# Coefficient transposes between the halves of the first MLP's first product, and two PSUM banks for the first product alone

## The reference

```python
def sq_relu_mlp(h, w1, w2):
    return jnp.square(jax.nn.relu(h @ w1)) @ w2

def second_block(x, ...):
    for layer in range(DEPTH):
        h = rms_norm_2(x, mix_norm_g[layer])
        ...
        x = x + sq_relu_mlp(rms_norm_2(x, ffn_norm_g[layer]), w_ff1[layer], w_ff2[layer])
```

## Time and profile before

| | us |
|---|---|
| median of 3 runs | 957.22 |
| lowest and highest run | 956.55, 960.41 |
| the profiled execution | 959.83 |
| its span, from first to last instruction | 958.0 |
| PE busy | 891.9 |
| DVE busy | 597.5 |
| ACT busy | 440.9 |
| POOL busy | 128.4 |

### The profile page before, as it was taken

How to read it: one execution, slowest core, us unless ns; L and a number is a source line. 1 busy time by engine, 2 the same in 40 slices (tenths; PEclk the granted TensorE clock), 3 DMA queues, 4 the chain that set the end, 5 groups by cost and what they waited for, 6 DMA issues and landing times.

```text
span 958.0 us, 12089 instructions
## 1 busy us (share of the span) xinstructions
PE 891.9 (93%) x5003; PEld 738.2 (77%) x5003; DVE 597.5 (62%) x704; ACT 440.9 (46%) x581; POOL 128.4 (13%) x73
## 2 busy tenths in 40 slices
PE   3999999898999999989999999998689989999997
PEld 2888778787887887787777888886677878888886
DVE  3595384675243765867697787886584565555453
ACT  5444375557853655343634444343126364444441
POOL 1000000211000011105054544441000000000000
PEclk9999999999999999579999999998779999999999
DMA  9625365363023642404545655554966555555521
GB/s 348 211 100 209 112 250 176 123 229 132 1 65 115 244 143 88 176 1 157 173 154 198 207 184 192 177 198 121 182 216 214 180 176 176 176 177 186 196 99 44
DMA packets 66784, 155.87 MB, mean 163 GB/s; under 512 B 2937, under 2 KB 6618, under 8 KB 66474
## 3 DMA queue, kind: packets, MB, share of 16 engines
q1 hardware_dynamic: 63424, 145.37, 45.0%
q0 software_dynamic: 2224, 7.67, 2.3%
q10 hardware_dynamic: 1082, 2.07, 1.0%
HBM read 146.70 MB, written 7.34 MB: 161 GB/s over the span
## 4 chain that ended last, share of the span: by engine, by line
PE 80%; DVE 10%; ACT 3%; issue 3%; DMA 2%; POOL 1%; ACTq 0%; DVEq 0%; POOLq 0%
PE bank L617 23%; PE bank L619 22%; PE bank L618 22%; PE bank L610 2%; PE bank L714 1%; DMA vrows<-in_vecs 1%; PE bank L872 1%; POOL rsh L1948 1%; DVE wlo L1385 1%; DVE wlo L1380 1%; DMA work<-x 1%; PE bank L755 1%; PE bank L687 1%; DVE aux L1558 1%; PE bank L976 1%
## 5 line engine op out<-in xcount | busy, mean ns | idle before, releaser
L1385 DVE TENSOR_TENSOR wlo<-ring,whi 128x2048 fp32r<-128x2048 f32 (+1 forms) x106 | 252.5, 2388 | 161.9 <-ACT whi L1062 161.8
L1062 ACT ACTIVATE whi<-ring 128x2048 fp32r<-128x2048 f32 (+1 forms) x106 | 202.3, 1910 | 234.9 <-PE bank L619 210.4
L617 PE MATMUL bank<-whi,hT_hi 128*128 128x512 f32 (+1 forms) x736 | 290.0, 394 | 5.8 <-DVE hT_lo L1368 4.1
L619 PE MATMUL bank<-whi,hT_lo 128*128 128x512 f32 (+1 forms) x736 | 287.7, 391 | 0.0
L618 PE MATMUL bank<-wlo,hT_hi 128*128 128x512 f32 (+1 forms) x736 | 287.5, 391 | 0.0
L617 PEld LDWEIGHTS bank<-whi,hT_hi 128*128 128x128 f32 x736 | 139.3, 189 | 35.2 <-DVE wlo L1385 2.8
L619 PEld LDWEIGHTS bank<-whi,hT_lo 128*128 128x128 f32 x736 | 139.2, 189 | 28.6
L618 PEld LDWEIGHTS bank<-wlo,hT_hi 128*128 128x128 f32 x736 | 139.3, 189 | 27.8
L617 PE MATMUL bank<-whi,hidT_hi 128*128 128x512 f32 x256 | 101.5, 396 | 1.1 <-DVE hidT_lo L1855 1.1
L619 PE MATMUL bank<-whi,hidT_lo 128*128 128x512 f32 x256 | 100.2, 392 | 0.0
L618 PE MATMUL bank<-wlo,hidT_hi 128*128 128x512 f32 x256 | 100.2, 391 | 0.0
(11 more groups left out here) (266 smaller groups left out, 998.6 us busy)
## 6 DMA issues: line engine op xcount, KB each, us to landing
ring<-in_w_ff SPq DMA_DIRECT2D x64, 1024.0 KB, 5.3
ring<-in_a_w_in SPq DMA_DIRECT2D x8, 1024.0 KB, 8.3
ring<-in_ple_gate_w SPq DMA_DIRECT2D x8, 1024.0 KB, 5.1
ring<-in_w_kv SPq DMA_DIRECT2D x8, 1024.0 KB, 6.4
ring<-in_b_w_in SPq DMA_DIRECT2D x8, 1024.0 KB, 5.1
ring<-in_w_in SPq DMA_DIRECT2D x6, 1024.0 KB, 5.6
ring<-in_w_glu SPq DMA_DIRECT2D x6, 1024.0 KB, 5.1
ring<-in_a_w_out SPq DMA_DIRECT2D x4, 1024.0 KB, 5.3
```

The costliest lines, as they stand in the source:

```text
L617: pe.matmul(bank_cols, high[:, at[0], at[1]], w_high, start=first, stop=False)
L619: return pe.matmul(bank_cols, low[:, at[0], at[1]], w_high, start=False, stop=last)
L1062: act.activation(whi[at], raw_rows(g), ACT.Copy).then_inc(high_made, 1)
L1385: dve.tensor_tensor(wlo[at], raw_rows(g), whi[at], ALU.subtract).then_inc(low_made, 1)
```

## The change

In the plan, the transposes of the hidden rows always go to banks 4 and 5, in both layers, and f1 to banks 6 and 7. In layer 0, wT goes to banks 4 and 5 as well (6 and 7 in turn 8), ahead of f1 in the count, and the taps to 4 and 5. PE runs the eight wT transposes between the two halves of f1, by the argument `between`, and the taps behind f1 as before. ACT copies wT out ahead of the two ReLUs, no longer behind the cast for f1's second half. DVE, POOL and SP keep their order.

```diff
--- before.py
+++ after.py
@@ -237,14 +237,16 @@
     for i in range(FB + 1):
         if i:
             for k in range(2):
-                u.add(("fT", layer, i - 1, k), "av")
+                u.add(("fT", layer, i - 1, k), "av", bank=4 + k)
+        if layer == 0 and i:
+            for k in range(2):
+                u.add(("wT", i - 1, k), "a", bank=(4 if i < FB else 6) + k)
         if i < FB:
-            gemm(u, ("f1", layer, i), 1, "v")
+            for t in range(NT):
+                u.add((("f1", layer, i), 0, t), "v", bank=6 + t)
         if layer == 0 and i:
-            u.add(("wT", i - 1, 0), "a")
-            u.add(("wT", i - 1, 1), "a")
-            u.add(("taps", i - 1, 0), "v")
-            u.add(("taps", i - 1, 1), "v")
+            for half in range(GH):
+                u.add(("taps", i - 1, half), "v", bank=4 + half)
     for k in range(4):
         u.add(("acc", layer, k), "v", bank=k)
     u.banks, u.turn = list(range(8)), 4
@@ -873,9 +875,12 @@
                                                         hid[:, t, c * P:(c + 1) * P], ident)
                             last.then_inc(pe_done, 1)
                     if i < FB:
-                        product(("f1", layer, i), 0, ("f1", layer, i), turned_by=("ffn", layer) if i == 0 else None)
+                        product(("f1", layer, i), 0, ("f1", layer, i), turned_by=("ffn", layer) if i == 0 else None,
+                                between=(lambda: s5_turn(n)) if layer == 0 and i else None)
+                    elif layer == 0:
+                        s5_turn(n)
                     if layer == 0 and i:
-                        s5_chunk(n)
+                        s5_taps_out(n)
                     if i:
                         for half in range(2):
                             g = 2 * order[("f2", layer, n)] + half
@@ -899,7 +904,7 @@
                             elif n < FB - 1:
                                 last.then_inc(f2_done, 1)
 
-            def s5_chunk(f):
+            def s5_turn(f):
                 pe.wait_ge(injects_made, f + 1)
                 for k in range(2):
                     b = begin(("wT", f, k))
@@ -907,6 +912,8 @@
                         at = (4 * k + g) * P
                         last = pe.transpose(b[:, g * P:(g + 1) * P], injects[:, f % 2, at:at + P], ident)
                     last.then_inc(pe_done, 1)
+
+            def s5_taps_out(f):
                 pe.wait_ge(readouts_made, f + 1)
                 banks = [begin(("taps", f, half)) for half in range(GH)]
                 for q in range(4):
@@ -1266,13 +1273,13 @@
                                            ACT.Copy).then_inc(high_turned, 1)
                     if i < FB:
                         refill(("f1", layer, i), 0)
+                    if layer == 0 and i:
+                        injects_out(i - 1)
+                    if i < FB:
                         for t in range(NT):
                             b = filled((("f1", layer, i), 0, t))
                             act.activation(hid[:, t, :], b[:, :], ACT.Relu).then_inc(relu_ready, 1)
-                    if i < FB:
                         refill(("f1", layer, i), 1)
-                    if layer == 0 and i:
-                        injects_out(i - 1)
                     if layer == 0 and i == FB:
                         act.preload_act_table_set("silu_and_others")
                         act.wait_ge(waves_turned, 1)
```

## The result

The changed kernel takes **962.08 us** (median of 10, 959.59 to 966.75) where the kernel before takes 956.42 (median of 10, 954.23 to 960.41): a ratio of 1.0056, 95% interval 1.0042 to 1.0070, so slower by 5.4 us (4.0 to 6.7). The forecast was +10.7. The direction and the wait that causes it are as forecast; the size is half.

The account below looks back on a forecast made before the run. PE is 80% of the chain, with DVE's loop behind each turn's 0.63 us wait. Turn 1's delay, five loops of 26.4 us and turn 7's wait end the MLP 10.7 us later: 957.22 becomes 967.9 us, range 962.0 to 971.5.

Parts of the forecast that it names:

- The seven waits of the taps go.: First MLP, turns 1 to 7: the taps' waits for DVE's product `hid`, 6.1 us in all, disappear.
- The hidden transposes wait for the tap copies.: Start of each following turn: PE's hidden transposes wait for DVE's tap copies, 2.0 us per turn in place of 0.63.
- I take the long ones, since POOL's start moves with E: DVE rows kept at their lengths beside POOL: inject pair 4.51 us (alone 2.07), weight part 3.10 (alone 2.25).
- only the weight part became short: DVE's weight part shortens by about 0.8 us in seven stretches: +5.1, 962.3 us; chance 0.10 together with rival (b).
- rival (b): Only wT's wait on L1855 binds: loop 25.46 us, end 6.0 later, 963.2 us; chance 0.10 with the short weight part.
- The loop of 26.4 us: One turn, from f1's second half issued to the same point next turn: 26.4 us, 1.24 more than 25.16.
- Turn 1, +3.84: wT waits about 2.8 us for DVE's low halves, so f1's second half is issued at 490.9 instead of 487.06.
- Turn 7, the wave step: DVE's 2.0 us more of wave products in turn 6 delay its low halves; wT waits under 1 us in turn 7.
- From E(7) on the same 19.89: From f1's second half issued in turn 7 to the end of L1855, DVE takes 19.89 us, as before.
- The clock: PE's clock behind turn 1's new wait of 2.8 us: nearer staying at 1.00; a fall costs about 2 us.
- (c): PE's clock falls every turn behind the 2.0 us waits, 2 us for each of six turns more: 980 us; chance 0.03.
- (d): Gains and waits cancel within 0.5%, DVE shorter by about 1 us in each loop: 961 us; chance 0.05.

Follow-up runs that it names:

- experiment 2: The changed kernel with DVE's two tap copies moved ahead of the inject products; 955.62 us, ratio 0.9994 to the kernel before.
- experiment 6: The changed kernel with POOL's products waiting for the second bank of f1, 2.7 us later; 980.19 us in one run.
- experiment 1: The changed kernel once more with no edit, for a second trace; 960.66 us, ratio 1.0041 to the kernel before.
- Experiment 7: The changed kernel's order with units paired by banks as in the kernel before; 963.71 us, ratio 1.0077 to the kernel before.
- experiment 3: The kernel before with taps between the halves of f2 (turns 1 to 7) and tap copies right behind the inject pair; 949.75 us, ratio 0.9933.
- experiment 8: The kernel of experiment 3 with the wave step of turn 7 moved behind the low halves of turn 8; 947.93 us, ratio 0.9915 to before.
- experiment 4: The changed kernel with POOL's readout products computed for one column of sixteen from the third chunk on; 948.73 us in one run.

## Why the forecast was right in its direction and wrong in its size

- *The seven waits of the taps go.* Right: none in turns 1 to 7.
- *The hidden transposes wait for the tap copies.* Right in place and count, seven times in turns 2 to 8. The size was wrong: 0.66 to 0.95 us, not 2.0. **The step that failed is the choice in the bounds, "I take the long ones, since POOL's start moves with E".** The reason is true, the conclusion does not follow from it. The term "start 13.24", in which a weight part of 3.10 us stood, measured 12.3 with one of 2.29. POOL's start does move, but not with DVE's: it went from E - 2.37 (511.47 less 513.84) to E - 2.46, yet it now stands at the end of the weight part ahead of it and no longer inside it, so its first product takes 2.69 instead of 3.57, and all that POOL does behind it is earlier against the next weight part. At the place where the exchange decides, 0.9 us is the difference between a wait and none.
- *The bound "only the weight part became short", 962.3.* This is the case that came in turns 2 to 6, and the median is 962.08. That the two lie 0.2 us apart is in part luck: the forecast counts from 957.22, the median of ten runs of before is 956.42, and the traces give +3.7 where the bound has +5.1. The text put 0.8 us on it for each loop, which at the end of the low halves gives +5.1; the trace shows +4.38 there. It had been given 0.10 together with rival (b), and stood at the range's low edge, since the forecast added it up for seven loops and took nothing off elsewhere. Of the two engines' rows that overlap, the forecast took the lengths of before as they were, without asking which instruction had waited for which.
- *The loop of 26.4 us.* Its other pieces held: with 12.32 in place of 13.24 the forecast's own sum is 25.5, and the loops from E(2) to E(6) are 25.54 to 25.57.
- *Turn 1, +3.84.* Right: +3.87. wT waits 2.60 us for the low halves, which stand behind the inject products on DVE; the forecast had 2.8. This is the largest single loss, and experiment 2 keeps it.
- *Turn 7, the wave step.* Right: wT waits 0.76 us for the low halves; E(6) to E(7) is 26.68 where 27.47 was forecast, shorter by the same 0.8.
- *From E(7) on the same 19.89.* It is 18.79. There the weight part takes 4.51 and the inject pair 2.06, in sum 6.57, where before had 3.10 + 4.5: the exchange again, in the order that turns 1 and 7 have.
- *The clock.* Right: turn 1's wait of 2.60 left it at 1.00. Not foreseen was that it returns sooner in turn 8, where the stretch behind the low halves is 0.66 us shorter than before.
- *Rivals.* (b), that only wT's wait binds, is wrong in its mechanism: in turns 2 to 6 wT has no wait. (c) did not occur in the change; experiment 6 shows it in three turns of six, behind waits of 2.8 us. (d), DVE shorter by about 1 us in each loop and a sum of +3.8, had 0.05 and is what the traces show: 0.8 to 1.1 us a loop and +3.7. Its condition, a difference within 0.5%, holds in experiment 1 (0.41%) and just fails in the first comparison (0.56%).
- *The rule weighed in the prediction*, the Trainium skill, Perfetto Trace Analysis, section Optimization Strategy: a repeated gap can mean too little buffer space. Experiment 7 bears it out in part, since the banks are worth 0.47 us a turn once the order is changed. Yet experiment 3 removes the same gap on the banks of before and reaches 951.1, the time by the rule alone (949.75), while experiment 2, on new banks and without that gap, stays at 955.62.

The clock's return in turn 8, in windows of 1 us some 3 us behind the start of the taps (659.71 and 663.36; the clock is the number behind POOL's busy time). Before:

```profile
662.70:663.70 1.00, 1.00 (x4) 0.81 (x3) 0.96 (x2) 0.00 (x0) 0.00 (x0) 0.50 0.72 272
```

And after, where it is at full speed:

```profile
666.40:667.40 1.00, 1.00 (x6) 0.84 (x5) 0.97 (x2) 0.00 (x0) 0.00 (x0) 1.00 0.68 262
```

What stays open: the times differ by 5.4 us (4.0 to 6.7) in the first comparison and by 3.9 (1.6 to 6.1) in the second, and the traces of the first MLP account for 3.7 and 3.9, which is a little under the first interval. The rest, if there is any, was not located. Why the stage behind the first MLP takes either of two times, 3 us apart, was not followed either.

## What to carry to other kernels

When a change gives one unit of work its own buffers, list who had them last for every other unit: here the taps were freed of one wait of 0.64 us and the hidden transposes were put behind a release that had 0.33 us of slack. Where two engines take turns on a shared resource, don't carry their row lengths over; take the lengths alone, lay the instructions out in their new times, and replay who waits for whom. And try moving the waiting step to a place where its input is long ready before giving it more buffers: that took the turn to 24.42 us, PE's own busy time, with no bank moved.

## What the runs showed of the hardware that was not expected

- With POOL's middle pair 0.9 us earlier against DVE's weight part (2.36 us ahead of it, before 1.48), that weight part takes 2.29 us instead of 3.10; with the pair 0.05 us ahead of it (experiment 6), the weight part and the inject pair together take 8.72 instead of 6.77. The total on DVE for these rows is 4.3 us with POOL nearly silent, 6.5 to 7.8 beside it, and 8.6 to 8.7 at the worst phase seen. In turns with the same phase it repeats within 0.1 us.
- The length of a wait does not settle what the clock does behind it. In experiment 6 it fell in the turns behind 2.79, 2.80 and 2.83 us (0.94 to 0.95 over the turn, with 1.5 to 1.6 us more of PE time) and stayed at 1.00 behind 2.71, 2.80 and 2.76. In turn 8 it was at 0.50 behind 2.40 us in experiment 8 and at 1.00 behind 3.17 us in experiment 4. Behind the 2.60 us of turn 1 it stayed in every kernel that has this wait.
- PE's busy time in a turn differs with the waits: 24.42 us when nothing waits, 24.50 to 24.66 with one wait; in the change the eight transposes behind the wait take 1.09 us where they take 1.04 in experiment 2.
